# Choosing the first group's rows in two halves, a last store on another queue, and row numbers before the second choice

## The reference, cut to what matters

```python
def _hier_moe(h, w_rg, b_rg, w_re, b_re, w_gate, w_up, w_down):
    hf = h.reshape(n * L, D)                      # 288 x 2048, after RMSNorm
    lg = hf @ w_rg + b_rg                         # 4 groups
    g_top = jnp.argmax(lg, axis=-1)
    p_top = softmax(lg)[g_top]
    le = (hf @ w_re + b_re).reshape(-1, 4, 4)
    top_v, top_i = lax.top_k(le[g_top], 2)        # best and second expert of the group
    pe = jax.nn.softmax(top_v, axis=-1)
    eidx = g_top * 4 + top_i
    gates = sum(one_hot(eidx, 16) * (p_top * pe))
    a = einsum('nd,edf->nef', hf, w_gate)         # 16 experts, 2048 -> 512
    b = einsum('nd,edf->nef', hf, w_up)
    hid = jax.nn.silu(a) * b * gates
    return einsum('nef,efd->nd', hid, w_down)     # 512 -> 2048

x = x + mix @ w_o
x = x + _hier_moe(_rms_norm(x, ln2_w), ...)
```

## Time and profile before

| | before |
|---|---|
| median of 3 runs | 1038.93 us (1036.13 to 1038.97) |
| profiled execution | 1041.82 us |
| its span, first to last instruction | 1039.9 us |
| PE busy | 943.9 us (91%), 4425 instructions |
| PEld busy | 456.8 us (44%) |
| DVE, ACT, POOL busy | 264.6, 135.4, 46.6 us |
| mean granted clock of TensorE | 0.971 |
| read from DRAM | 329.71 MB, 329 GB/s over the span |

### The profile page before, as it was taken

One profiled execution on the slowest core, in us unless ns is written; L12 is line 12 of the kernel. 1 busy time (PEld: TensorE's weight loads), 2 busy tenths in 40 slices (PEclk: granted clock), 3 DMA queues, 4 the chain that ended last, 5 costly groups with the idle time before them and its releaser, 6 DMA issues.

```text
span 1039.9 us, 10198 instructions
## 1 busy us (share of the span) xinstructions
PE 943.9 (91%) x4425; PEld 456.8 (44%) x4425; DVE 264.6 (25%) x377; ACT 135.4 (13%) x301; POOL 46.6 (4%) x85
## 2 busy tenths in 40 slices
PE   6999999999999999999977899996889778997895
PEld 3444434444445666777754334432343223432331
DVE  1105999673143330101133101101011100111001
ACT  4201111121024441000010010001000010100000
POOL 0002100101110000000000000000000000000000
PEclk8999999999999999999987999999999899999998
DMA  9955699954959997419537999999999999999991
GB/s 343 380 187 190 226 404 400 355 189 151 294 225 350 352 363 284 146 45 407 197 135 304 382 373 421 420 422 423 421 420 423 420 422 422 420 422 422 412 396 79
DMA packets 81041, 339.19 MB, mean 326 GB/s; under 512 B 7332, under 2 KB 11278, under 8 KB 56624
## 3 DMA queue, kind: packets, MB, share of 16 engines
q1 hardware_dynamic: 61263, 296.45, 71.8%
q10 hardware_dynamic: 15808, 33.84, 8.7%
q0 software_dynamic: 3920, 8.19, 2.2%
HBM read 329.71 MB, written 12.24 MB: 329 GB/s over the span
## 4 chain that ended last, share of the span: by engine, by line
PE 72%; DMA 24%; DVE 1%; issue 1%; ACT 1%; POOL 0%; SPq 0%; POOLq 0%; DVEq 0%
PE PS L872 70%; DMA ring<-in_w_up 10%; DMA ring<-in_w_gate 4%; DMA ring<-in_w_down 2%; DMA aux<-in_w_up 2%; DMA X<-in_cache_k 2%; DMA aux<-in_w_down 2%; DMA ring<-in_w_in 1%; PE PS L953 1%; DMA x_scr<-Z 1%; DMA X<-x_scr,pidx 1%; PE PS L1153 1%; DVE Z L1763 0%; DVE HT L1763 0%; PE PS L1043 0%
## 5 line engine op out<-in xcount | busy, mean ns | idle before, releaser
L872 PE MATMUL PS<-ring,HT 128*128 128x512 f32 (+2 forms) x1184 | 375.4, 606 | 11.6 <-DMA ring<-in_w_up 6.8
L872 PE MATMUL PS<-ring,Z 128*64 128x512 f32 (+2 forms) x912 | 240.9, 588 | 26.8 <-DMA ring<-in_w_up 7.1
L872 PEld LDWEIGHTS PS<-ring,HT 128*128 128x128 f32 (+2 forms) x1184 | 141.4, 157 | 210.2 <-issue 209.1
L872 PEld LDWEIGHTS PS<-ring,Z 128*64 128x64 f32 (+1 forms) x912 | 84.3, 141 | 150.5 <-issue 145.6
L872 PE MATMUL PS<-HT,ring 128*128 128x288 f32 x512 | 128.4, 409 | 0.6 <-issue 0.6
L872 PEld LDWEIGHTS PS<-HT,ring 128*128 128x128 f32 x512 | 96.0, 190 | 33.4 <-issue 8.2
L872 PE MATMUL PS<-aux,Z 128*64 128x512 f32 (+2 forms) x208 | 72.5, 525 | 3.3 <-DMA ring<-in_w_down 1.7
L872 PE MATMUL PS<-Z,X 128*128 128x256 f32 x128 | 41.2, 455 | 10.7 <-DMA X<-x_scr,pidx 5.0
L872 PEld LDWEIGHTS PS<-Z,X 128*128 128x128 f32 x128 | 32.7, 325 | 27.1 <-issue 13.0
L1823 DVE TENSOR_TENSOR Z<-Z,PS 128x512 f32<-128x512 f32 x8 | 5.5, 687 | 144.5 <-PE PS L872 144.5
L1763 DVE TENSOR_TENSOR Z<-PS,ln2R 128x512 f32<-128x512 f32 x16 | 11.1, 692 | 121.6 <-PE PS L872 121.6
(11 more groups left out here) (208 smaller groups left out, 541.9 us busy)
## 6 DMA issues: line engine op xcount, KB each, us to landing
ring<-in_w_gate SPq DMA_DIRECT2D x27, 2048.0 KB, 21.3
ring<-in_w_up SPq DMA_DIRECT2D x25, 2048.0 KB, 22.0
ring<-in_w_down SPq DMA_DIRECT2D x23, 2048.0 KB, 22.5
ring<-in_w_in ACTq DMA_DIRECT2D x12, 2048.0 KB, 16.5
ring<-in_w_o SPq DMA_DIRECT2D x8, 2048.0 KB, 12.9
ring<-in_cache_v SPq DMA_DIRECT2D x8, 1536.0 KB, 7.6
ring<-in_cache_v SPq DMA_DIRECT2D x32, 384.0 KB, 8.6
aux<-in_w_gate SPq DMA_DIRECT2D x5, 2048.0 KB, 24.7
```

The costliest lines, as they stand in the source:

```text
L872: return pe.matmul(out, lhsT, rhs, start=start, stop=stop, skip_group_check=True)
```

## The change

The change has three pieces. The first group's choice is cut by places instead of by chunks alone: parts 0 to 3 make places 0 to 127 for four chunks each, parts 4 to 7 places 128 to 255. Each part is four products with 128 columns of `SR`. Parts 0 to 2 come before gate 0, parts 3 and 4 before gate 1, parts 5 to 7 and the gate table before up 0. The store of the last 128 columns moves from GpSimd to SyncE, ahead of loads 5 and 6, behind a wait for `rows_moved`. The row numbers, with their wait for `idx_done`, move ahead of the second choice on VectorE.

```diff
-    FIRST_BANKS = (7, 2, 5, 1)
+    FIRST_BANKS = (7, 2, 5, 1, 7, 5, 7, 5)
@@ SyncE, experts
                     elif i == 5:
+                        sp.wait_ge(rows_moved, 14)
+                        sp.dma_start(x1_scr[0:SEQ, D - P:D].rearrange("(c p) d -> p c d", p=P),
+                                     z[:, 0:2, D - P:D]).then_inc(x1_last, 16)
+                        sp.dma_start(x1_scr[SEQ:TOK, D - P:D], z[0:NS, 2, D - P:D]).then_inc(x1_last, 16)
                         sp.wait_ge(wo_done, 16)
@@ GpSimd
         pool.wait_ge(pstored, 16 * (1 + DEC_B))
-        pool.wait_ge(rows_moved, 14)
-        pool.dma_start(x1_scr[0:SEQ, D - P:D].rearrange("(c p) d -> p c d", p=P),
-                       z[:, 0:2, D - P:D]).then_inc(x1_last, 16)
-        pool.dma_start(x1_scr[SEQ:TOK, D - P:D], z[0:NS, 2, D - P:D]).then_inc(x1_last, 16)
         pool.wait_ge(rows_ready, 1)
@@ TensorE, first_select
             if j >= 4:
-                pe.wait_ge(htg_moved, j - 3)
-            select(0, j, FIRST_BANKS[j % 4])
+                pe.wait_ge(htg_moved, (1, 3, 5, 6)[j - 4])
+            t0 = j // 4 * 2 * CAP
+            for i in range(4):
+                c = 4 * (j % 4) + i
+                q0 = c // RUN * RUN * P
+                ins = mm(PS[:, FIRST_BANKS[j], i * P:(i + 1) * P], XG[0][:, q0 + c % RUN:q0 + RUN * P:RUN],
+                         SR[:, t0:t0 + 2 * CAP], True, True)
+            ins.then_inc(htg_turned, 1)
@@ TensorE, experts
                 if starts:
-                    for j in range(5):
+                    for j in range(3):
                         first_select(j)
-                    pe.wait_ge(htg_moved, 4)
+                    pe.wait_ge(htg_moved, 2)
                 up(k, 0, 0, g0_used)
                 if starts:
-                    for j in range(5, 8):
+                    for j in range(3, 5):
                         first_select(j)
-                    pe.wait_ge(htg_moved, 8)
+                    pe.wait_ge(htg_moved, 4)
                 up(k, 0, 1, gate_done)
                 if starts:
+                    for j in range(5, 8):
+                        first_select(j)
                     first_gates()
+                    pe.wait_ge(htg_moved, 8)
@@ VectorE
         step(dve.tensor_reduce(m4, work, AX.X, ALU.max))
+        dve.wait_ge(idx_done, 1)
+        rows_of(0)
         first_of(second, work, m4, d4, NG)
         rs = R[:, 364:412].rearrange("p (k g v) -> p k g v", g=NG, v=4)
         step(dve.tensor_tensor(rs, top, second, ALU.add))
         dve.tensor_tensor(rs, rs, each(oh, NG), ALU.mult).then_inc(sel_ready, 1)
-        dve.wait_ge(idx_done, 1)
-        rows_of(0)
@@ VectorE, after the gates' chain
             dve.wait_ge(htg_turned, j + 1)
-            pair_out(0, j, FIRST_BANKS[j % 4])
+            c0, t0 = 4 * (j % 4), j // 4 * 2 * CAP
+            dve.tensor_tensor(HTG[0][:, c0:c0 + 4, t0:t0 + 2 * CAP],
+                              PS[:, FIRST_BANKS[j], :].rearrange("p (c t) -> p c t", c=4),
+                              ln2R[:, c0:c0 + 4].unsqueeze(2).to_broadcast([P, 4, 2 * CAP]),
+                              ALU.mult).then_inc(htg_moved, 1)
```

## The result

The changed kernel takes 1045.60 us in the median (1044.22 to 1047.86, 4 runs) where the kernel before takes 1037.53 (1034.50 to 1038.97, 4 runs beside it). The ratio is 1.008 with an interval of 1.0054 to 1.0106: 8 us slower, between 5.6 and 11.0. The two profiled executions are 6.0 apart (1047.86 and 1041.82), their spans 6.1 (1046.0 and 1039.9). TensorE runs 32 products and 32 weight loads more: 948.4 us busy with 4457 instructions, 463.0 us of weight loads.

A forecast was written before the change was run, and what follows sets the result against it. TensorE was taken to bound the kernel from the first gather to the load issue at 612.40, DMA after it; gather +2.0 and choice +4.5 gave +6.5 us on a 1038.93 median, so 1045.4, range 1041.0 to 1050.0.

The forecast's parts named there:

- What bounds the kernel: TensorE from the first gather's landing to the load issue at 612.40, then DMA at a fixed rate of 419 GB/s.
- Rival D: Early releases of weight loads count after all: with the gather at −0.2 the end moves −1, median 1037.9; chance 0.04.
- The store: On SyncE it lands at about 541.5; loads 5 and 6 leave 2.65 us later, their own lateness covered by 28 us.
- Row numbers: VectorE writes them from 545.94, 0.17 us gained; the first selection matrix ends at 551.5, hidden under the gather.
- The gather: Late loads lie on the first gather: bounds −0.2 and +4.0 us, taken as landing at 555.2, +2.0.
- the sum with the full 9.9: A gather issued anywhere inside a load pays the full wait of 9.9 us, making the sum 2 us longer.
- The choice: On TensorE, 64 weight loads at a 0.232 us beat plus 0.2, 15.05 instead of 10.58 us: +4.5.
- Rival A: Choice's weight loads priced by columns, so halves cost half; total −1.8 to +0.4 us, median 1037.1 to 1039.3; chance 0.09.
- B: Smaller loss: gather not caught by loads, choice's weight loads at 0.21 us; total +2.9, median 1041.8; chance 0.10.
- The sum: Gather +2.0 and choice +4.5 give +6.5 us at the end, median 1045.4.
- C: TensorE's clock falls in the second quarter too, +1.8 us; with the gather at +4.0 total +10.3, median 1049.2; chance 0.13.

The follow-up runs named there:

- choice_only: Changed kernel with the store back on GpSimd and the row numbers back behind the second choice; ratio to the kernel before 1.0054 (1.0034 to 1.0074).
- store_only: Kernel before with only the store of the last columns moved to SyncE ahead of loads 5 and 6; ratio 1.0018 (0.9999 to 1.0038).
- packed: Changed kernel with the choice's weight loads from 128 neighbouring floats instead of every fourth; ratio to the kernel before 0.9988 (0.9967 to 1.0010).
- stride2: Changed kernel with the choice's weight loads from every second float instead of every fourth; one execution, no timed ratio, product to load 17 67.4 us.
- loads_held: Changed kernel with loads 5 and 6 held back until the first gather has landed; ratio to the kernel before 1.0048 (1.0029 to 1.0067).
- table_early: Kernel before with the gate table's product moved ahead of gate 1, its two turns left behind it; ratio 0.9953 (0.9933 to 0.9973).

## Why the prediction was right, point by point

*What bounds the kernel.* TensorE up to load 17, DMA behind it: right, as the last column of the table bears out. Rival D, that early releases count, falls with choice_only: there loads 9 and 10 left 0.6 earlier after the product than before (567.08 − 545.18 = 21.90 against 22.5), and the end came later by the same 6.2 as load 17.

*The store.* Loads 5 and 6 were to leave at 539.55; they left at 539.42. The store was quicker than its bound (1.9 and 1.7 us instead of 2.5), which changed nothing.

*Row numbers.* VectorE stands still for 1.26 us and writes them from 545.77 (545.94 forecast):

```profile
545.77 0.17 DVE L1720 TENSOR_SCALAR pidx<-PS 128x8 int32<-128x8 f32 x1 [1.26 <-PE PS L872]
...
550.25 0.98 DVE L1765 TENSOR_SCALAR Z<-X,gates 128x64 f32<-128x64 f32 x4
```

The selection matrix ends at 551.23 (551.5 forecast), hidden under the gather.

*The gather.* Forecast +2.0, taken near the middle of −0.2 and +4.0. Counted from the product it is +1.9 in the changed kernel, +1.7 in store_only. That the middle came true was luck. The time is no mean of a free and a busy gather: the first packet comes 4.0 us after the issue instead of 1.7, when the loads have nearly drained, and the rest takes its 3.9 as without them. So the sum with the full 9.9, which the prediction set against its own, is not what happened. The rule that it took from the Trainium skill, "DMA: Bandwidth & Descriptors", section "Queues, rings and completion order", agrees with the start if its descriptor is what the trace counts as a packet: 210 of the loads, 13 for each of the 16 engines, ran before the first of the gather. It does not give the 9.9.

*The choice.* Forecast 15.05, measured 15.42. The beat was right; each of the three stretches takes 0.13 to 0.22 more than its beats (5.79, 3.93 and 5.70 against 5.57, 3.71 and 5.57), where I had allowed 0.2 in all. Half clock did not matter for it, as forecast: the 24 loads of the first stretch take 5.67 at 0.52 granted, (5.67 − 0.33) / 23 = 0.232 each. Rival A, the price by columns, falls with the packed loads, and B with the beat and the late gather. The rule of the Trainium skill, "TensorE: Matmul & The Clock Gate", section "LDWEIGHTS (loading the stationary operand)", does not hold for a stride of four (0.232), while its 128 / 1.2 = 107 ns fits the packed 0.111.

*The sum.* +6.5 forecast; +6.7 at load 17 from the product, +6.0 between the profiled executions, +8 in the timed ratio with an interval that holds 6.5. 1045.4 was forecast and 1045.6 measured, but part of this closeness is chance: the median before came down by 1.4 with a fourth run.

*What was not foreseen* is that the clock is part of the price. The prediction kept the third quarter at its 8.82 in any case and gave C only the second quarter. Behind the gate table the third quarter runs from 7.00 (packed) to 9.94 (choice_only); in the changed kernel it came out nearly as before, by luck, so the sum did not suffer. What decides between them was not settled: the gate table takes the same 2.70 in the kernel before, the changed one, packed and stride2, and only in the last two the clock stayed full; and choice_only runs the same parts in the same times as the changed kernel, yet its clock fell earlier.

## What to carry to other kernels

Find the last transfer that had to wait for an engine. Here what moved that one moved the end, and releasing earlier ones earlier was worth nothing. Cutting a product into narrower ones multiplies its weight loads: look at what two loads take back to back, and at the stride they read with, before counting on half the time. A load put off by 2.5 us for the sake of a small store lands on the next transfer that everything waits for, so look at what lies in the queue where it now falls.

## What the runs showed of the hardware that I had not expected

- A weight load of 128 x 128 floats keeps a beat of 0.111 us packed, 0.118 from every second float, 0.232 from every fourth and 0.237 from every eighth.
- The same gate table (2.70 to 2.73 us, of which TensorE stands still for 1.5) was followed by a third quarter at a granted clock of 0.81 behind gate 1 (before), of 0.80, 0.72 and 0.73 behind slow parts (changed, choice_only, loads_held), and of 1.00 behind quick parts (packed, stride2); without it the clock stayed full (table_early).
- A gather issued while loads were under way moved nothing for 4 us while the loads moved 1.70 MB, and then had DMA nearly to itself. With DMA empty it moved nothing for 1.7 us either (loads_held).
